# Softplus sums of a stick-breaking attention as 0/1 products of split parts, and its causal mask moved from GpSimd to VectorE

## The reference

```
z = (q @ k.T) / sqrt(64)
strict = s < t
log_keep = where(strict, log_sigmoid(-z), 0)
later = reverse_cumsum(log_keep) - log_keep
w = where(strict, exp(log_sigmoid(z) + later), 0)
o = w @ v
```

## Time and profile before

| what | value |
|---|---|
| runs | 902.0, 901.87, 902.0 us, median 902.0 |
| span of the profiled execution, first to last instruction | 900.7 us |
| around the span, against the median of the runs | 1.3 us |
| PE busy | 888.3 us, 99% of the span |
| DVE, ACT, POOL busy | 571.0, 496.2, 136.0 us |
| granted TensorE clock, mean | 1.000 |

### The profile page before, as it was taken

How to read it: one execution, slowest core, us unless ns; L and a number is a source line. 1 busy time by engine, 2 the same in 40 slices (tenths; PEclk the granted TensorE clock), 3 DMA queues, 4 the chain that set the end, 5 groups by cost and what they waited for, 6 DMA issues and landing times.

```text
span 900.7 us, 15634 instructions
## 1 busy us (share of the span) xinstructions
PE 888.3 (99%) x6451; PEld 821.5 (91%) x6451; DVE 571.0 (63%) x824; ACT 496.2 (55%) x771; POOL 136.0 (15%) x151
## 2 busy tenths in 40 slices
PE   8999999999999999999999999999999999999998
PEld 8999999889999988788899988999999899998886
DVE  4556554878888746666767797765467655554542
ACT  5576864556656634566776764423454565554330
POOL 6011101611111100133443110000100011110000
PEclk9999999999999999999999999999999999999999
DMA  7843364665665566346544546542345656656560
GB/s 279 275 155 118 95 227 150 232 207 181 199 199 179 188 210 214 131 169 242 182 141 144 160 133 177 155 135 77 115 140 191 187 168 202 193 187 204 181 200 23
DMA packets 132594, 156.33 MB, mean 174 GB/s; under 512 B 9353, under 2 KB 106028, under 8 KB 132268
## 3 DMA queue, kind: packets, MB, share of 16 engines
q1 hardware_dynamic: 125844, 151.78, 51.9%
q10 hardware_dynamic: 6680, 3.56, 1.3%
HBM read 153.08 MB, written 2.24 MB: 172 GB/s over the span
## 4 chain that ended last, share of the span: by engine, by line
PE 83%; DVE 8%; DMA 3%; ACT 3%; issue 1%; POOL 1%; SPq 0%; ACTq 0%; POOLq 0%
PE ps L1979 72%; PE ps L1934 4%; PE ps L2010 3%; DVE wl L828 2%; PE ps L1931 2%; PE ps L2235 2%; DVE gv L862 1%; DVE gkq L862 1%; DMA U<-blocks 1%; DMA raw<-in_w_in 1%; DMA blocks<-last 1%; DVE mt L1267 1%; DMA Yc<-inverses 1%; ACT wh L1426 1%; DMA inverses<-Y 0%
## 5 line engine op out<-in xcount | busy, mean ns | idle before, releaser
L828 DVE TENSOR_TENSOR wl<-raw,wh 128x1024 fp32r<-128x1024 f32 (+1 forms) x275 | 326.4, 1205 | 190.0 <-ACT wh L1426 189.9
L1979 PE MATMUL ps<-xh,wh 128*128 128x256 f32 x1280 | 357.3, 282 | 0.7 <-ACT xh L1474 0.7
L1979 PE MATMUL ps<-xh,wl 128*128 128x256 f32 x1280 | 350.6, 277 | 0.0
L1426 ACT ACTIVATE wh<-raw 128x1024 fp32r<-128x1024 f32 (+1 forms) x292 | 286.6, 1024 | 115.4 <-PE ps L1979 93.0
L1979 PE MATMUL ps<-xl,wh 128*128 128x256 f32 x1280 | 348.3, 277 | 0.0
L1979 PEld LDWEIGHTS ps<-xh,wh 128*128 128x128 f32 x1280 | 238.9, 188 | 4.5 <-issue 1.4
L1979 PEld LDWEIGHTS ps<-xh,wl 128*128 128x128 f32 x1280 | 238.8, 188 | 0.0
L1979 PEld LDWEIGHTS ps<-xl,wh 128*128 128x128 f32 x1280 | 238.0, 188 | 0.3
L669 POOL TENSOR_TENSOR wl<-raw,wh 128x1024 fp32r<-128x1024 f32 (+1 forms) x17 | 44.2, 2600 | 81.6 <-ACT wh L1426 81.3
L1979 PE MATMUL ps<-wh,f2L 128*128 128x512 f32 x128 | 49.8, 389 | 0.0
L1979 PE MATMUL ps<-wl,f2H 128*128 128x512 f32 x128 | 49.8, 389 | 0.0
(11 more groups left out here) (334 smaller groups left out, 1363.8 us busy)
## 6 DMA issues: line engine op xcount, KB each, us to landing
raw<-in_w_in SPq DMA_DIRECT2D x55, 1024.0 KB, 5.1
raw<-in_w_up SPq DMA_DIRECT2D x38, 1024.0 KB, 5.2
raw<-in_w_down SPq DMA_DIRECT2D x26, 1024.0 KB, 5.0
raw<-in_w_out SPq DMA_DIRECT2D x8, 1024.0 KB, 5.1
raw<-in_w_proj_fox SPq DMA_DIRECT2D x4, 1024.0 KB, 5.1
raw<-in_w_proj_gdn SPq DMA_DIRECT2D x4, 1024.0 KB, 5.1
raw<-in_w_conv_branch SPq DMA_DIRECT2D x4, 512.0 KB, 3.4
raw<-in_w_att_branch SPq DMA_DIRECT2D x4, 512.0 KB, 3.3
```

What stands on the lines that cost most here:

```text
L828: e.tensor_tensor(L, R, H.bitcast(F32), ALU.subtract).then_inc(lo.sem)
L1426: e.activation(tile_of(WH, u)[:, k:kc, :], tile_of(RAW, u)[:, k:kc, :], ACT.Copy).then_inc(hi.sem)
L1979: k = e.matmul(o, l, r, start=opens, stop=done and n == ends[c], skip_group_check=True)
```

## The change

- `TRI` and `ones` are declared float32r (they hold only 0 and 1). Where the second block still uses `ones` it reads it as float32.
- sp is split: ACT copies it rounded into `spH` (new step `sH`, it takes the place of `ex` in memory), DVE subtracts to get `spL` (new step `sL`, in place of sp). The C block becomes four float32r products for each s: the triangle on 384 columns and the ones on 128 columns, for spH and for spL.
- A constant `MKA` holds 0 where a key is allowed and -1e30 where it is masked. POOL makes it with the late constants. DVE adds it as z leaves PSUM (`z0` moves from ACT to DVE, as a tensor_tensor add). With z at -1e30, softplus and the weight are 0 by themselves.
- POOL's whole attention task (both selects) is gone.
- The ticks within a round are now: DVE `z0` 2, ACT Abs/Exp/Ln 3, DVE `s` 7, ACT `sH` 8, DVE `sL` 9, PE C block 11, DVE `d` 12, ACT `w` 15, PE O block 18, ACT `oh` 18, DVE `ol` 21.

```diff
-        ones = fixed("ones", [P, P])
-        TRI = fixed("tri", [P, P])
+        ones = fixed("ones", [P, P], F32R)
+        TRI = fixed("tri", [P, P], F32R)
...
+        MKA = reg("mka", [P, 384], 20)
+        spH, spL = ([reg(f"sp{k}{i}", [P, 384], 25 + 1.5 * (2 * n + i), F32R) for i in range(2)] for n, k in ((1, "H"), (2, "L")))
...
             def late_constants():
                 yield from pause(12)
+                memset(MKA[:], 0.0)
+                for b in (0, 256):
+                    select(MKA[:, b:b + P], ALU.is_gt, NEG, 0, [[1, P]], -1)
...
-            def attention(s):
-                def diag(ap):
-                    return ap[:].rearrange("p (b t) -> p b t", b=3)[:, 0::2, :]
-
-                for i in range(4):
-                    yield from pause(6)
-                    v = diag(att[2][s])
-                    e.wait_ge(*att_dve[s]("s", i))
-                    in_turn()
-                    signals(e.affine_select(out=v, in_=v, compare_op=ALU.is_gt, fill=0.0, base=0, pattern=[[0, 2], [1, P]],
-                              channel_multiplier=-1), att_pool[s])
-                    yield from pause(5)
-                    v = diag(att[3][s])
-                    e.wait_ge(*att_dve[s]("d", i))
-                    in_turn()
-                    signals(e.affine_select(out=v, in_=v, compare_op=ALU.is_gt, fill=NEG, base=0, pattern=[[0, 2], [1, P]],
-                              channel_multiplier=-1), att_pool[s])
-                    yield from pause(9)
...
             def attention(s):
                 zs, ex, sp_, d = (att[n][s] for n in range(4))
-                C, O, o = PS[4 + 2 * s], PS[7], 64 * s
+                z, C, O, o = PS[3 + 2 * s], PS[4 + 2 * s], PS[7], 64 * s
                 for i in range(4):
+                    yield
+                    e.wait_ge(*cst("mka"))
+                    e.wait_ge(*att_pe[s]("z", i))
+                    e.tensor_tensor(zs[:], z[:, 0:384], MKA[:], ALU.add).then_inc(att_dve[s].sem)
                     yield from pause(5)
                     e.wait_ge(*att_act[s]("ln", i))
                     e.scalar_tensor_tensor(sp_[:], zs[:], 0.0, ex[:], ALU.max, ALU.add).then_inc(att_dve[s].sem)
-                    yield from pause(6)
+                    yield from pause(2)
+                    e.wait_ge(*att_act[s]("sH", i))
+                    e.tensor_tensor(spL[s][:], sp_[:], spH[s][:].bitcast(F32), ALU.subtract).then_inc(att_dve[s].sem)
+                    yield from pause(3)
                     e.wait_ge(*att_pe[s]("c", i))
...
                 for i in range(4):
-                    yield
-                    e.wait_ge(*att_pe[s]("z", i))
-                    copy(zs[:], z[:, 0:384]).then_inc(me.sem)
-                    e.wait_ge(*me("z0", i))
+                    yield from pause(2)
+                    e.wait_ge(*att_dve[s]("z0", i))
                     e.activation(ex[:], zs[:], ACT.Abs).then_inc(me.sem)
...
-                    yield from pause(14)
-                    e.wait_ge(*att_pool[s]("kd", i))
+                    yield from pause(5)
+                    e.wait_ge(*att_dve[s]("s", i))
+                    copy(spH[s][:], sp_[:]).then_inc(me.sem)
+                    yield from pause(7)
+                    e.wait_ge(*att_dve[s]("d", i))
                     e.activation(d[:], d[:], ACT.Exp).then_inc(me.sem)
...
                     if i:
-                        e.wait_ge(*ac("z0", i - 1))
+                        e.wait_ge(*dv("z0", i - 1))
...
-                    e.wait_ge(*po("ks", i))
+                    e.wait_ge(*dv("sL", i))
                     if i:
                         e.wait_ge(*dv("d", i - 1))
-                    mul(C[:, 0:256], TRI[:], sp_[:, 0:256], True, False)
-                    mul(C[:, 128:256], ones[:], sp_[:, 256:384], False, True)
-                    mul(C[:, 256:384], TRI[:], sp_[:, 256:384], True, True).then_inc(me.sem)
+                    for n, sp_ in enumerate((spH[s], spL[s])):
+                        mul(C[:, 0:384], TRI[:], sp_[:], n == 0, False)
+                        k = mul(C[:, 128:256], ones[:], sp_[:, 256:384], False, n == 1)
+                    k.then_inc(me.sem)
```

More of the change, by code:

```diff
@@ L301, in two_blocks @@
         mm = steps("mm_end", "part")
-        cst = steps("constants", "id0", "id", "np", "on", "tri0", "tri", "uf0", "uf", "ui0", "ui1", "ui", *(f"uv{k}" for k in range(6)),
+        cst = steps("constants", "id0", "id", "np", "on", "tri0", "tri", "mka0", "mka1", "mka", "uf0", "uf", "ui0", "ui1", "ui", *(f"uv{k}" for k in range(6)),
                     "ul0", "ul", "ob0", "ob", "mk0", "mk1", "mk", "ml0",
@@ L328, in two_blocks @@
         att_pe = [steps(f"att_pe{i}", "z", "c", "o") for i in range(2)]
-        att_act = [steps(f"att_act{i}", "z0", "ab", "ex", "ln", "w", "oh") for i in range(2)]
-        att_dve = [steps(f"att_dve{i}", "s", "d", "ol") for i in range(2)]
-        att_pool = [steps(f"att_pool{i}", "ks", "kd") for i in range(2)]
+        att_act = [steps(f"att_act{i}", "ab", "ex", "ln", "sH", "w", "oh") for i in range(2)]
+        att_dve = [steps(f"att_dve{i}", "z0", "s", "sL", "d", "ol") for i in range(2)]
         gc = steps("gate_conv", "g")
@@ L618, in constants @@
                 memset(npow[:], -0.5)
-                memset(ones[:], 1.0)
-                memset(TRI[:], 1.0)
-                select(TRI[:], ALU.is_ge, 0.0, 0, [[-1, P]], 1)
+                memset(ones[:].bitcast(F32), 1.0)
+                memset(TRI[:].bitcast(F32), 1.0)
+                e.wait_ge(*before)
+                signals(e.affine_select(out=TRI[:], in_=TRI[:].bitcast(F32), compare_op=ALU.is_ge, fill=0.0, base=0, pattern=[[-1, P]],
+                          channel_multiplier=1), cst)
             def late_constants():
                 yield from pause(12)
+                memset(MKA[:], 0.0)
+                for b in (0, 256):
+                    select(MKA[:, b:b + P], ALU.is_gt, NEG, 0, [[1, P]], -1)
                 memset(UF[:], 1.0)
@@ L767, in gpsimd @@
             side.add(late_constants())
[L768 to L772, removed]
+            for u in range(U_UP):
                 unit(u)
@@ L1493, in attention @@
             def attention(s):
-                zs, ex, _, d = (att[n][s] for n in range(4))
-                z, O, o = PS[3 + 2 * s], PS[7], 64 * s
+                zs, ex, sp_, d = (att[n][s] for n in range(4))
+                O, o = PS[7], 64 * s
                 me = att_act[s]
                 for i in range(4):
-                    yield
-                    e.wait_ge(*att_pe[s]("z", i))
-                    copy(zs[:], z[:, 0:384]).then_inc(me.sem)
-                    e.wait_ge(*me("z0", i))
+                    yield from pause(2)
+                    e.wait_ge(*att_dve[s]("z0", i))
                     e.activation(ex[:], zs[:], ACT.Abs).then_inc(me.sem)
@@ L1512, in attention @@
                     copy(oH[o:o + 64, i, :], O[o:o + 64, 0:256]).then_inc(me.sem)
-                    yield from pause(2)
+                    yield from pause(3)
             def conv_mix_high(i):
@@ L2078, in attention @@
             def attention(s):
-                _, _, sp_, d = (att[n][s] for n in range(4))
+                d = att[3][s]
                 z, C, O, o = PS[3 + 2 * s], PS[4 + 2 * s], PS[7], 64 * s
                 rows = slice(o, o + 64)
-                me, ac, dv, po = att_pe[s], att_act[s], att_dve[s], att_pool[s]
+                me, ac, dv = att_pe[s], att_act[s], att_dve[s]
                 for i in range(4):
@@ L2127, in small @@
                 mul(ps4[0:NH, 0:128], G_lf[:, 0, :], UF[:], True, True)
-                mul(ps4[0:NH, 128:256], G_lf[:, 0, :], ones[:], True, False)
+                mul(ps4[0:NH, 128:256], G_lf[:, 0, :], ones[:].bitcast(F32), True, False)
                 mul(ps4[0:NH, 128:256], G_lf[:, 1, :], UF[:], False, True)
```

## The result

The changed kernel takes 907.0 us (median of 5 runs, 906.1 to 908.7) against 902.0 for the kernel before: a ratio of 1.0052, 95% interval 1.0041 to 1.0063. A second set gave 906.7 against 902.6, ratio 1.0053 (1.0036 to 1.0070). It is slower by 4 to 5 us, and both intervals exclude 1; the forecast was +1.3 us and the range ended at 905.4.

A forecast was written before the change was run, and what follows sets the result against it. PE, busy 99% of the span, was taken to bound the kernel, with operand readiness at the C block: -2.5 (PE), -0.7 (old wait), +3.4 + 1.05 + 0.1 (new waits) = +1.35 us, so 903.3 us; range 900.6 to 905.4.

The forecast's parts named there:

- PE's gain: C block on PE: 1.13 us instead of 1.75 for both s, 0.62 saved a block, 2.5 us in four rounds.
- the smaller prices beside it: Short 128-column product in the C block: 0.058 us (0.8 us more saved in all), or 81 ns by the skill (0.5 more).
- The old wait of 0.7: PE's wait for POOL's select ahead of the second round's C block; it goes, -0.7 us.
- The wait of the second round: PE waits 3.4 us for `sL` ahead of the C block, where it waited 0.7 before.
- The third round's: PE waits 1.05 us for `sL` ahead of the third round's C block.
- The sum: PE's gain, old wait and new waits: -2.5, -0.7, +3.4 + 1.05 + 0.1 = +1.35 us.
- the case that it falls in the 3.4 us wait: Rival, second round: PE's clock falls in the wait, +1.45 us on top, +2.8 in all, 904.8; chance 0.08.
- In the fourth round `w`: ACT's table loads, gate and `high` precede `w`; PE waits 0.1 us at the O block.
- a lag that piles up over rounds 3 and 4: Rival: 0.1 us more per DVE/ACT step costs 0.3 in round 2, 0.5 in round 3, 0.3 at `w`; +2.4, 904.4; chance 0.26.
- The faster one: Rival: `sL` is ready in round 2, no wait comes, PE's gain stands whole: -2.5 - 0.7, 898.8; chance 0.12.
- one bound: Lower bound of the forecast 903.3: 128 columns at 0.058 (-0.8), hops 0.05 cheaper in eight steps (-0.4), given as 901.9.

The follow-up runs named there:

- early: The changed kernel with the same instructions in another order, its steps moved ahead on DVE and ACT; 900.2 us, ratio 0.9976.
- mask_only: Against the kernel before: the mask moves to DVE, softplus stays unsplit and the C block float32; 903.3 us, ratio 1.0007.
- split_only: Against the kernel before: softplus split and C block float32r, with ACT's copy and POOL's two selects kept; 907.8 us, ratio 1.0055.
- again: The changed kernel as it is, run once more for a second trace; 906.7 us, ratio 1.0053.
- after_settle: The changed kernel with one extra float32 product behind the last round's O block, result not used; 907.2 us, ratio 1.0059.
- low_first: The changed kernel with two pieces of DVE's other work (second half of the weight split, ycL) one tick later; 905.1 us, ratio 1.0031.
- filler: The changed kernel with 15 dummy float32 products on PE ahead of its wait in the second round; 905.0 us, ratio 1.0027.
- early_settle: The early version with one extra float32 product behind the last round's O block, result not used; 899.2 us, ratio 0.9965.

## Why the prediction was wrong

**What held.** PE's gain: I wrote 1.13 us a block and 0.62 saved; it is 1.09 and 0.66 in the first round and in every round of *early*, near the 0.11 us that I took for the short product and not near the smaller prices beside it. Behind a wait the block takes 1.20 at the full clock; there I had overlooked that the float32 block behind the old wait took 2.02 and not 1.75. The old wait of 0.7 went. The wait of the second round was to be 3.4 us and is 3.25, through the chain I followed: z0 behind `oL`, the ACT steps, `high`, wl, ycL, s, wl, spL, in that order. The third round's was to be 1.05 and is 0.99. *mask_only*, *split_only* and *early* show what brings it: the mask alone adds 0.4 us of wait, the split alone makes one of 3.1 us, and moving the steps removes all.

**The step that failed.** The sum had the clock at 1.00 and gave the case that it falls in the 3.4 us wait a chance of 0.08. So the clock stood in the sum at nothing. It fell in all five traces with a wait of 2.2 us or more in the second round (the changed kernel, *again*, *after_settle*, *split_only*, *low_first*), in 20 of 24 executions by their mean clock, and in none of the others. The price in the rival was nearly right: +1.45 us written, 1.6 measured by *filler* against *again*. I took the longest wait of before, 1.7 us at the full clock, for half an answer, and gave the unknown beyond it almost no weight. Even with its price the rival ends at 904.8, 2 us short of the medians; the rest is in the next two terms. The rule that I cited from the Trainium skill (TensorE: Matmul & The Clock Gate, Part 1), that activity releases the clock, was the thing to weigh; these traces agree with it: with PE idle for 3.2 us the clock fell to half in *again*, with dummy products in that time it stayed at 1.00 in *filler*.

**A term too small.** In the fourth round `w` makes PE wait 0.47 us where I had 0.1. ACT's chain was the right one (two table loads, the gate, 3.05 us of `high`, then Exp). The O block behind this wait also takes 0.4 us more, 1.20 to the next product instead of 0.81 (*again*):

```profile
116.80 1.28 PE L1925 MATMUL ps<-at,vS 128*64 128x256 f32 x8 [0.47 <-ACT at L1500]
118.00 0.39 PE L1970 MATMUL ps<-xh,wh 128*128 128x256 f32 x1
```

**A term that was missing.** The pace of the products is in no step. It works in both directions: the 40 products behind a C block gain 0.18 us in three of the changed kernel's four rounds (the third stays slow), 0.5 in all, and the long stretch loses 1.7 when it is slow. In the trace *again*, where it was fast, the span is 2.8 us above before. My +1.35, +1.6 for the clock, +0.4 for `w`, -0.3 for waits and blocks a little shorter than written, -0.5 for the pace behind the C blocks, make 2.55. That this comes so near is partly luck. The part of the trace that the change touches is longer by 3.6 us: from the second product of the first round (46.50 us before, 46.29 in *again*) to the last product of 256 columns ahead of a long run of 512-column ones (309.58 and 312.94) PE takes 263.1 us before and 266.65 in *again*, and the rest of the span gives 0.8 back. So about 1 us is missing from the 2.55: 0.4 of it is the O block just shown, the other 0.6 was not traced. By the same measure *mask_only* takes 263.55, *filler* 265.05, *early* 260.6 in both traces, *early_settle* 259.6 in both, and the changed kernel, with its long stretch slow, 268.1. Between the spans of *again* and of the first trace of the changed kernel, 6.3 us above before, lie 3.6 us; the 3.3 us of slow pace named above would make up nearly all of them. The runs lie between: the medians 4 to 5 us above before.

**The rival that a part of the runs bore out** was the one that ends on the slower side by the clock. The other slower one, a lag that piles up over rounds 3 and 4, did not happen beyond the 0.4 us at `w`. The faster one, 3.2 us below before, is near what the change gives with its steps in a better order: *early* is 2.4 and 3.1 us below before in its two sets. Of the numbers of that forecast, one bound slips: 903.3 less 0.8 and 0.4 is 902.1, not 901.9, which changes nothing here.

**A version that beats both.** *early_settle* at 0.9957 and 0.9965 of before, by the medians 4.4 and 3.6 us faster than it and some 8 us faster than the changed kernel. By its trace the gain has three parts: no waits (0.7 against before), C blocks (2.6), the pace behind them (0.7), 4.0 together, less 0.4 for the O block with the extra product in it (1.22 us instead of 0.81).

What stays open: why two paces exist, what picks one, and why the clock stayed whole in four executions of 24 with a long wait. It was not tried to put the extra product in the other long stretches.

## What to carry to other kernels

When a product gets its operands by two more short steps on other engines, ask first what stands ahead of those steps in the queue of each engine: here the same instructions, with the steps of the attention moved ahead by a few ticks, made the difference between 4.0 to 5.0 us slower and 2.4 to 3.1 us faster by the medians. A wait of the busiest engine is worth more than its length: behind waits of 2.2 us and more the clock fell to half in these traces, and that cost 1.6 us where it was measured. So a new wait that is longer than any in the trace needs such a price in the forecast with more than a small chance. And if a kernel's times come in steps of about a microsecond, count the start-to-start time of its most frequent instruction before looking for a cause in the change.

## What the runs showed of the hardware

- The granted clock fell to half (1.2 GHz) behind a wait of PE of 2.2 us (*low_first*) and behind those of 3.1 to 3.25, in five traces of five, each time for 3.4 us. Waits of 1.1 us at the same place (*mask_only*) and of 1.7 us near 190 us in the traces did not do it. Dummy products in the wait kept it at 1.00 (*filler*). By the mean clock it fell in 20 of 24 executions with such waits.
- The fall does not come with the wait but 0 to 1.7 us behind its end: in the changed kernel it meets the first product; in *low_first* the first product is still at full speed (0.28 us to the next); in *again* six products of the block are, up to 74.16, and in *split_only* the whole block (73.53 to 74.73).
- Float32r products with 256 columns follow each other at 113.3 or 117.8 ns, whole stretches long, at the same granted clock. Behind a float32 C block of 128 rows it was the slow pace in 16 stretches of 16, behind the float32r one in *early* the fast one in four of four, in the changed kernel in three of four.
- A float32r product of 384 columns and one of 128 take 0.29 us together, 0.23 and 0.06 from start to start (*early*). Their 512 columns at the 0.229 us of one long product would be 0.06 less:

```profile
70.54 0.39 PE L1924 MATMUL ps<-spL,tri 128*128 128x384 f32 x1
70.77 0.22 PE L1924 MATMUL ps<-spL,ones 128*128 128x128 f32 x1
70.83 0.39 PE L1924 MATMUL ps<-spH,tri 128*128 128x384 f32 x1
```
